# A two-layer hybrid trunk on one core: Toeplitz blocks written from their diagonal on, first GLU weights loaded early, S5 carries kept apart

## The chip, the cores and the metric

The program runs on one core of a Trainium2 chip. The metric is the device time of one execution in microseconds (us); lower is better. Three runs of the kernel before gave 1280.75, 1279.62 and 1279.68 us: median 1279.68 us.

The core has a matrix engine (PE, TensorE), a vector engine (DVE, VectorE), a scalar engine (ACT, ScalarE), a general engine (POOL, GpSimd) and SP (SyncE), which here only issues DMAs. ACT issues DMAs too, from the same instruction stream as its arithmetic. All DMAs share 16 DMA engines. The engines run their own instruction lists and wait for each other at semaphores.

## What is computed

x has 512 tokens of 1024 values. Layer 0 is an S5 mixer and a SwiGLU block, layer 1 a retention mixer and a SwiGLU block, with a norm before each. The change touches the S5 mixer alone:

```python
lam_bar = jnp.exp(lam * step)                      # 64 groups x 64 complex states
b_bar = ((lam_bar - 1.0) / lam)[..., None] * b
bu = jnp.einsum('blgn,gpn->blgp', uf, b_bar)       # uf: normed x, 64 groups of 16
_, states = lax.associative_scan(combine, (a, bu), axis=1)   # s[t] = lam_bar*s[t-1] + bu[t]
y = jnp.einsum('gnp,blgp->blgn', c, states).real + d * uf
y = jax.nn.gelu(y.reshape(bsz, seq, D_MODEL))
y = y * jax.nn.sigmoid(y @ glu_w + glu_b)
```

## The kernel before

**Tiling.** The 512 tokens are 64 chunks of 8 steps (`CH`, `STEPS`). The 64 groups sit as 32 pairs `j`, two groups to the 128 partitions. Within a chunk, the output is a product of the chunk's inputs `u` with a block Toeplitz matrix `toep`; what came before the chunk enters by the chunk's first state, `states`, times tables `r_tc`. So y = u x toep (`y_inputs`, L680) + states x tables (`y_states`, L660), both on PE, accumulated in one PSUM bank for each four pairs (k = 0 to 7).

**Toeplitz blocks.** PE makes the nonzero taps of four pairs at a time (`strips(k)`, L609 and L612). ACT copies them to `strip` in `w_raw` (`strip_out(k)`), behind seven steps of zeros that POOL wrote at the start (L1684). A row block r (16 partitions) of `toep` is the strip shifted by r steps. `toeplitz_half(queue, part, half)` (L427 to L436) waits until the two strips of a part are copied and issues eight DMAs, r = 0 to 7, each from 16 partitions to 16 partitions of SBUF with 4096 bytes a partition. SP does this for half 0, ACT for half 1, for four parts (0 to 3): 32 DMAs on each. `toep_loaded[part]` counts both halves.

**Scan.** DVE scans the 64 chunk states as 8 segments of 8 (L1368 to L1381; `seg_done` 1), carries the ends of the segments on (L1384 to L1400, 3 operations a segment; `seg_done` 2) and adds the carried ends to the seven inner states of each later segment, in four quarters of the pairs (L1403 to L1424, eight operations of 392 elements a quarter; `scan_done` 1 to 4). The powers for that come from POOL (`segment_powers`, `lift_ready`), between two of its seven table blocks (`tc_ready`).

**Order.** Each engine's list is written out by hand. ACT's list around the change: strips 0 and 1 out, DMAs of part 0, strips 2 and 3, eight copies to `xT`, DMAs of part 1, strips 4 and 5, DMAs of part 2, strip 6, the load of the Gelu table (L1007), strip 7, DMAs of part 3, then four Gelus (L1017), four `g_hi` copies, the first split of GLU weights `w_hi` (`split_weights(0, 0)`), and the second four of each. PE's list: y_inputs 0 to 3, y_states of quarter 0, y_inputs 4 and 5, y_states of quarter 1, transposes of y 0 to 3 (L672), y_inputs 6 and 7, y_states of quarters 2 and 3, transposes 4 to 7, and then the GLU products (L709 to L711), from which on PE goes through the rest of the network. The strips and the GLU weights share `w_raw`, so SP loads the first weights when all Toeplitz DMAs of a slot have landed. PSUM copies of the chunk states (`s5_input_out`) are written with the chunk as the innermost index, 256 bytes from element to element.

## Time and profile before

| what | us |
|---|---|
| median of three runs | 1279.68 |
| profiled execution | 1278.21 |
| its span on the core | 1276.4 |
| PE busy (matmul) | 1240.6 (97% of the span) |
| DVE busy | 671.7 (53%) |
| ACT busy | 462.0 (36%) |
| POOL busy | 64.8 (5%) |

The profiled execution is 1.8 us longer than its span: that lies before the first and after the last instruction. Busy time counts arithmetic only. A DMA that ACT or SP issues is not busy time, but the engine does nothing else while it issues; the timeline shows these under ACTq and SPq. "[1.46 <-DVE ...]" behind a row is the time that the engine stood idle before it and what ended that. The chain of waits follows the end of the program back from what released it to what released that; its rows are not a sum over an engine but one path in time. The granted clock is the share of full speed at which PE was let run: 1.00 is 2.4 GHz, 0.50 is 1.2 GHz.

### The profile page before, as it was taken

The numbers are of one execution on the slowest core, as the hardware profiler recorded it, in microseconds if no ns is written. First come the engines' busy times: TensorE is split into PE (matmuls) and PEld (weight loads), VectorE is DVE, ScalarE is ACT, GpSimd is POOL, SyncE is SP. The second block draws the span as 40 slices with busy tenths as digits, with TensorE's granted clock in tenths as the row PEclk, the third lists the DMA queues.
The fourth block names the chain that finished last, engine by engine and source line by source line (L and its number), as shares of the span: only waits on it lengthen the run. The fifth ranks groups of instructions, "written<-read, shape, count | busy, mean of one in ns | idle before, by whom it ended". The sixth has DMA issues, their size and how long they took to land.

```text
span 1276.4 us, 16013 instructions
## 1 busy us (share of the span) xinstructions
PE 1240.6 (97%) x6277; PEld 1034.5 (81%) x6277; DVE 671.7 (53%) x785; ACT 462.0 (36%) x486; POOL 64.8 (5%) x82
## 2 busy tenths in 40 slices
PE   3889999999999999999999999999999999999998
PEld 3778888888888888888888888888888888888886
DVE  8997754344444444646655465634454444444443
ACT  5635433333333333333333333422333333332232
POOL 6940000000000000000000000000000000000000
PEclk9999999999999999999999999999999999999999
DMA  5373333332312334323232133233232323323331
GB/s 115 100 144 123 99 99 99 99 99 90 105 58 90 105 90 138 107 66 107 66 99 83 57 107 96 69 96 93 74 119 80 102 94 99 99 68 90 93 110 66
DMA packets 141039, 121.03 MB, mean 95 GB/s; under 512 B 5720, under 2 KB 132880, under 8 KB 141008
## 3 DMA queue, kind: packets, MB, share of 16 engines
q1 hardware_dynamic: 138832, 116.40, 29.5%
q10 hardware_dynamic: 2176, 4.20, 1.7%
q8 instruction: 22, 0.36, 0.1%
q14 instruction: 9, 0.07, 0.0%
HBM read 114.29 MB, written 2.10 MB: 91 GB/s over the span
## 4 chain that ended last, share of the span: by engine, by line
PE 94%; ACTq 2%; ACT 2%; DMA 1%; DVE 1%; issue 0%; SPq 0%; DVEq 0%
PE bank L709 27%; PE bank L711 27%; PE bank L710 27%; PE bank L809 2%; PE bank L808 2%; PE bank L807 2%; ACTq L434 2%; DMA s<-in_x_dram 1%; PE bank L835 1%; PE bank L837 1%; PE bank L836 1%; PE bank L846 1%; PE bank L820 0%; PE bank L821 0%; ACT s_states L900 0%; PE bank L537 0%
## 5 line engine op out<-in xcount | busy, mean ns | idle before, releaser
L709 PE MATMUL bank<-u_hi,w_hi 128*128 128x512 f32 x960 | 374.9, 391 | 0.0
L711 PE MATMUL bank<-u_hi,w_lo 128*128 128x512 f32 x960 | 373.6, 389 | 0.0
L710 PE MATMUL bank<-u_lo,w_hi 128*128 128x512 f32 x960 | 373.5, 389 | 0.0
L1186 DVE TENSOR_TENSOR w_lo<-w_raw,w_hi 128x2048 fp32r<-128x2048 f32 x112 | 256.4, 2290 | 165.7 <-ACT w_hi L900 165.6
L900 ACT ACTIVATE w_hi<-w_raw 128x2048 fp32r<-128x2048 f32 x112 | 214.0, 1910 | 319.1 <-PE bank L711 314.0
L709 PEld LDWEIGHTS bank<-u_hi,w_hi 128*128 128x128 f32 x960 | 180.2, 188 | 37.8 <-issue 0.7
L710 PEld LDWEIGHTS bank<-u_lo,w_hi 128*128 128x128 f32 x960 | 180.2, 188 | 37.6 <-issue 0.5
L711 PEld LDWEIGHTS bank<-u_hi,w_lo 128*128 128x128 f32 x960 | 180.2, 188 | 37.5
L709 PE MATMUL bank<-h_hi,w_hi 128*128 128x512 f32 x352 | 136.9, 389 | 0.0
L710 PE MATMUL bank<-h_lo,w_hi 128*128 128x512 f32 x352 | 136.9, 389 | 0.0
L711 PE MATMUL bank<-h_hi,w_lo 128*128 128x512 f32 x352 | 136.9, 389 | 0.0
L1176 DVE TENSOR_TENSOR tmp<-bank,tmp 128x512 f32<-128x512 f32 (+3 forms) x60 | 38.0, 634 | 97.1 <-PE bank L711 94.3
L1092 ACT ACTIVATE tmp<-tmp 128x512 f32<-128x512 f32 x44 | 27.7, 632 | 138.9 <-DVE tmp L1525 138.0
L1525 DVE TENSOR_TENSOR tmp<-bank,tmp 128x512 f32<-128x512 f32 x44 | 30.0, 691 | 91.2 <-PE bank L711 90.7
L711 PEld LDWEIGHTS bank<-h_hi,w_lo 128*128 128x128 f32 x352 | 66.1, 188 | 13.8
L710 PEld LDWEIGHTS bank<-h_lo,w_hi 128*128 128x128 f32 x352 | 66.1, 188 | 13.7
L709 PEld LDWEIGHTS bank<-h_hi,w_hi 128*128 128x128 f32 x352 | 66.1, 188 | 13.7
L1451 DVE TENSOR_TENSOR xT<-bank,xT 128x512 f32 (+1 forms) x24 | 16.6, 692 | 92.5 <-PE bank L711 92.5
L1042 ACT ACTIVATE u_hi<-xT,vecs (+1 forms) x24 | 17.3, 721 | 124.4 <-DVE xT L1451 124.4
L709 PE MATMUL bank<-y_hi,w_hi 128*128 128x512 f32 x128 | 49.9, 390 | 0.0
L710 PE MATMUL bank<-y_lo,w_hi 128*128 128x512 f32 x128 | 49.8, 389 | 0.0
L711 PE MATMUL bank<-y_hi,w_lo 128*128 128x512 f32 x128 | 49.8, 389 | 0.0
(220 smaller groups left out, 1321.6 us busy)
## 6 DMA issues: line engine op xcount, KB each, us to landing
w_raw<-in_ret_w_qkvg_dram SPq DMA_DIRECT2D x24, 1024.0 KB, 4.9
w_raw<-in_ffn_w_gate_dram SPq DMA_DIRECT2D x22, 1024.0 KB, 5.2
w_raw<-in_ffn_w_up_dram SPq DMA_DIRECT2D x22, 1024.0 KB, 5.1
w_raw<-in_ffn_w_down_dram SPq DMA_DIRECT2D x32, 704.0 KB, 4.1
w_raw<-in_ret_w_o_dram SPq DMA_DIRECT2D x8, 1024.0 KB, 5.1
w_raw<-in_s_glu_w_dram SPq DMA_DIRECT2D x4, 1024.0 KB, 5.5
s<-in_x_dram ACTq DMA_DIRECT2D x8, 256.0 KB, 8.5
s_w<-in_x_dram SPq DMA_DIRECT2D x1, 2048.0 KB, 7.6
```

What stands on the lines that cost most here:

```text
L434: queue.dma_start(toep[N * r:N * r + N, half, part, :, :, :].rearrange("p t j n -> p (t j n)"), strip[row:row + N, part % 2, first:first + ...
L709: pe.matmul(o, w_hi[w][:, w_cols], hi, start=first, stop=False)
L710: pe.matmul(o, w_hi[w][:, w_cols], lo, start=False, stop=False)
L711: return pe.matmul(o, w_lo[w][:, w_cols], hi, start=False, stop=end)
L807: pe.matmul(o, a_hi, w_hi[s][:, cols], start=(kk == 0), stop=False)
L808: pe.matmul(o, a_hi, w_lo[s][:, cols], start=False, stop=False)
L809: mm = pe.matmul(o, a_lo, w_hi[s][:, cols], start=False, stop=(kk == KT - 1))
L900: return act.activation(o, i, ACT.Copy, scale=scale)
L1092: act.activation(sig[:, m, :], sig[:, m, :], ACT.Silu).then_inc(gate_ready, 1)
L1176: return dve.tensor_tensor(o, a, b, ALU.mult)
L1186: dve.tensor_tensor(w_lo[s][:, :], w_raw[:, s, :], w_hi[s][:, :].bitcast(F32), ALU.subtract).then_inc(w_lo_ready[s], 1)
L1525: dve.tensor_tensor(sig[:, m, :], bank[m][:, :], rs, ALU.mult).then_inc(bank_free[m], 1)
```

## The change

It has these parts.

1. `toeplitz_half` sends the strip from the diagonal on: row block r takes 8 - r steps, 4096 - 512 r bytes a partition. What lies before the diagonal is zeroed by seven DMAs of SP from a row of zeros that POOL writes (`zeros`, in slot 0 of `w_raw`), before the token load. The strips now all lie in slot 1.
2. Slot 0 of `w_raw` is free once the zeros have landed, so SP loads the first GLU weights there right behind the token load. ACT's first split moves up to between the table load and strip 7.
3. DVE keeps the carried segment ends in a tile of its own, `carries`. ACT copies the first of them (`carry0_ready`; DVE waits for it before the lift) and copies the other six back into `states` (`ends_ready`; PE waits for it before `y_states`).
4. The lift of a quarter is one product of 392 elements, one of 784 and two additions of 784. POOL makes its two tables (`lift_pair`), two more operations of 224 elements in `segment_powers`.
5. PE: y_inputs 4 ahead of y_states of quarter 0; y_inputs 6 and 7 ahead of transposes 0 to 3. DVE's making of `step64` moves ahead of the scan. `s5_input_out` writes four pairs side by side, 16 bytes at a stretch.

ACT's list from behind the DMAs of part 2 to the first Gelu, before (`s_1` is `toep`, `s_3` holds `carries`, the 32x8x64 copies are `strip_out`):

```order
L900 ACTIVATE w_raw<-bank 32x8x64 [waits bank_full4]
L1007 ACT_TABLE_LOAD
L1007 ACTIVATE small<-eps 128x1
L900 ACTIVATE w_raw<-bank 32x8x64 [waits bank_full5]
L434 DMA s_1<-w_raw 16x1024 [waits bank_free5,bank_free4]
L434 DMA s_1<-w_raw 16x1024 x7
L1017 ACTIVATE y_chunk<-bank 128x4x8x16 [waits bank_full6]
```

The same place now, up to the second of the eight DMAs of part 3:

```order
L920 ACTIVATE s_3<-s_states 128x4x16 [waits seg_done]
L920 ACTIVATE w_raw<-bank 32x8x64 [waits bank_full4]
L1028 ACT_TABLE_LOAD
L1028 ACTIVATE small<-eps 128x1
L920 ACTIVATE w_hi<-w_raw 128x2048 [waits w_loaded0]
L920 ACTIVATE s_states<-s_3 128x6x32 [waits seg_done]
L920 ACTIVATE s_states<-s_3 128x6x32
L920 ACTIVATE w_raw<-bank 32x8x64 [waits bank_full5]
L444 DMA s_1<-w_raw 16x1024 [waits bank_free5,bank_free4]
L444 DMA s_1<-w_raw 16x896
```

Four instructions came in ahead of the DMAs of part 3: the copy of the first carry, the split of the weights, and the two copies of the carried ends.

PE's list from y_states of quarter 1 to y_inputs 6, before (L672 transposes a finished y, L680 is `y_inputs`, L660 `y_states`):

```order
L660 MATMUL bank<-s_tc,s_states 64x128 [waits scan_done]
L660 MATMUL bank<-s_tc,s_states 64x128 x31
L672 MATMUL bank<-ident,y_chunk 128x128 [waits bank_free6,bank_free7]
L672 MATMUL bank<-ident,y_chunk 128x128 x3
L672 MATMUL bank<-ident,y_chunk 128x128 [waits bank_free7]
L672 MATMUL bank<-ident,y_chunk 128x128 x3
L672 MATMUL bank<-ident,y_chunk 128x128 [waits bank_free2,bank_free3]
L672 MATMUL bank<-ident,y_chunk 128x128 x3
L672 MATMUL bank<-ident,y_chunk 128x128 [waits bank_free3]
L672 MATMUL bank<-ident,y_chunk 128x128 x3
L680 MATMUL bank<-s_1,s_u 64x128 [waits bank_free4,toep_loaded3]
L680 MATMUL bank<-s_1,s_u 64x128 x7
```

And now, from y_inputs 4 on (L699 is `y_inputs`, L679 `y_states`, L691 the transposes):

```order
L699 MATMUL bank<-s_1,s_u 64x128 [waits toep_loaded2,seg_done]
L699 MATMUL bank<-s_1,s_u 64x128 x7
L679 MATMUL bank<-s_tc,s_states 64x128 [waits scan_done,ends_ready]
L679 MATMUL bank<-s_tc,s_states 64x128 x31
L699 MATMUL bank<-s_1,s_u 64x128 x8
L679 MATMUL bank<-s_tc,s_states 64x128 [waits scan_done,ends_ready]
L679 MATMUL bank<-s_tc,s_states 64x128 x31
L699 MATMUL bank<-s_1,s_u 64x128 [waits bank_free4,toep_loaded3]
L699 MATMUL bank<-s_1,s_u 64x128 x7
L699 MATMUL bank<-s_1,s_u 64x128 [waits bank_free5]
L699 MATMUL bank<-s_1,s_u 64x128 x7
L691 MATMUL bank<-ident,y_chunk 128x128 [waits bank_free6,bank_free7]
```

The wait for part 3 of the Toeplitz blocks now stands ahead of the transposes 0 to 3 as well.

The diff (the new semaphores, the waits of PE for `ends_ready` and `toep_zeroed`, and the renamed views of `step64` and `carry_tmp` are left out):

```diff
-        strip = w_raw[0:4 * N, :, 0:(2 * STEPS - 1) * PART * N].rearrange("p s (t j n) -> p s t j n", t=2 * STEPS - 1, j=PART)
-        scan_tmp = r_3[:, 4096:8192]
+        strip = w_raw[0:4 * N, 1, :].rearrange("p (s t j n) -> p s t j n", s=2, t=STEPS, j=PART)
+        zeros = w_raw[0:N, 0, 0:(STEPS - 1) * PART * N]
+        lift_pair = powers[:, :, :, :].rearrange("p r t j -> p (r t j)")[:, 0:2 * (SEG - 1) * J] \
+            .rearrange("p (i r j) -> p i r j", i=SEG - 1, r=2)
+        carries = r_3[:, 4096:4544].rearrange("p (q s r j) -> p q s r j", q=4, s=SEG - 1, r=2)
+        carry_diff = r_3[:, 4544:4768].rearrange("p (q s j) -> p q s j", q=4, s=SEG - 1)
+        lifted_diff = r_3[:, 4768:5160].rearrange("p (s i j) -> p s i j", s=SEG - 1, i=SEG - 1)
+        lifted = r_3[:, 5160:5944].rearrange("p (s i r j) -> p s i r j", s=SEG - 1, i=SEG - 1, r=2)
+        seg = states[:, 1:CH + 1, :, :].rearrange("p (s i) r j -> p s i r j", s=SEG)
+        seg_ends = seg[:, :, SEG - 1, :, :].rearrange("p s r (q j) -> p s q r j", q=4)
 
...
                 queue.wait_ge(bank_free[b], fill + 1)
             row = 2 * N * (part // 2) + N * half
             for r in range(STEPS):
-                first = STEPS - 1 - r
-                queue.dma_start(toep[N * r:N * r + N, half, part, :, :, :].rearrange("p t j n -> p (t j n)"),
-                                strip[row:row + N, part % 2, first:first + STEPS, :, :].rearrange("p t j n -> p (t j n)")
+                queue.dma_start(toep[N * r:N * r + N, half, part, r:, :, :].rearrange("p t j n -> p (t j n)"),
+                                strip[row:row + N, part % 2, 0:STEPS - r, :, :].rearrange("p t j n -> p (t j n)")
                                 ).then_inc(toep_loaded[part], 16)
 
         @block.sync
                 n = vec.shape[0] // P
                 sp.dma_start(vec_rows[col:col + n, :], vec.rearrange("(k p) -> k p", p=P)).then_inc(vecs_loaded, 16)
 
+            sp.wait_ge(zeros_set, 1)
+            b, fill = S5_AT[("u", 7)]
+            sp.wait_ge(bank_full[b], fill + 1)
+            for r in range(1, STEPS):
+                cols = r * PART * N
+                sp.dma_start(toep[N * r:N * r + N, :, :, 0:r, :, :].rearrange("p h q t j n -> p (h q) (t j n)"),
+                             repeated(zeros[:, 0:cols], 1, 2 * NPART)).then_inc(toep_zeroed, 16)
+
             b, fill = S5_AT[("tb", 4 * NTAB - 1)]
             sp.wait_ge(bank_full[b], fill + 1)
             sp.dma_start(x_tok, x[0].rearrange("(t p) d -> p t d", p=P)).then_inc(x_loaded, 16)
 
-            sp.wait_ge(pads_zeroed, 1)
+            sp.wait_ge(toep_zeroed, 16 * (STEPS - 1))
+            load_unit(0, 0, glu_v[:, :, 0:256], KT, 256)
             for part in range(NPART):
                 toeplitz_half(sp, part, 0)
-            for s in range(2):
-                for part in (s, 2 + s):
-                    sp.wait_ge(toep_loaded[part], 16 * 2 * STEPS)
-                load_unit(s, 0, glu_v[:, :, 256 * s:256 * s + 256], KT, 256)
+            for part in range(NPART):
+                sp.wait_ge(toep_loaded[part], 16 * 2 * STEPS)
+            load_unit(1, 0, glu_v[:, :, 256:512], KT, 256)
             for s in range(2):
                 load_unit(s, 1, glu_v[:, :, 512 + 256 * s:768 + 256 * s], KT, 256)
 
...
             pe.wait_ge(seg_done, 2)
-            y_states(0, 0)
             pe.wait_ge(toep_loaded[2], 16 * 2 * STEPS)
             y_inputs(4)
+            y_states(0, 0)
             y_inputs(5)
             y_states(1, 1)
-            for k in range(4):
-                y_transposed(k)
             pe.wait_ge(toep_loaded[3], 16 * 2 * STEPS)
             y_inputs(6)
             y_inputs(7)
+            for k in range(4):
+                y_transposed(k)
             y_states(2, 4)
             y_states(3, 5)
             for k in range(4, 8):
...
             def s5_input_out(k):
                 ps, free = s5_full("b", k)
-                copy(states[:, 1:CH + 1, :, JB * SLOT[k]:JB * SLOT[k] + JB].rearrange("p c r j -> p j r c"),
-                     ps[:, :].rearrange("p (j r c) -> p j r c", j=JB, r=2)).then_inc(free, 1)
+                copy(states[:, 1:CH + 1, :, JB * SLOT[k]:JB * SLOT[k] + JB],
+                     ps[:, :].rearrange("p (j r c) -> p c r j", j=JB, r=2)).then_inc(free, 1)
...
-            act.wait_ge(pads_zeroed, 1)
             toeplitz_half(act, 0, 1)
             strip_out(2)
             strip_out(3)
...
             strip_out(4)
             strip_out(5)
             toeplitz_half(act, 2, 1)
+            act.wait_ge(seg_done, 1)
+            copy(carries[:, :, 0], seg_ends[:, 0]).then_inc(carry0_ready, 1)
             strip_out(6)
             act.activation(small[:, 25:26], eps[:, :], ACT.Gelu_apprx_tanh)
+            split_weights(0, 0)
+            act.wait_ge(seg_done, 2)
+            for ri in range(2):
+                copy(seg[:, 1:SEG - 1, SEG - 1, ri, :].rearrange("p s (q j) -> p s q j", q=4),
+                     carries[:, :, 1:SEG - 1, ri, :].rearrange("p q s j -> p s q j")).then_inc(ends_ready, 1)
             strip_out(7)
             toeplitz_half(act, 3, 1)
 
...
 
-            dve.wait_ge(lift_ready, 1)
+            dve.wait_ge(lift_ready, 2)
             rotation(step8, seg_powers[:, :, 0, :])
+            last_lift = seg_powers[:, :, SEG - 1, :].rearrange("p r (q j) -> p r q j", q=4)
+            step(dve.tensor_copy(step64[:, 0], repeated(last_lift[:, 0], 2, 2)))
+            step(dve.tensor_copy(step64[:, 1, :, 0], last_lift[:, 1]))
+            step(dve.tensor_scalar(step64[:, 1, :, 1], last_lift[:, 1], -1.0, None, ALU.mult))
+            settle()
 
             dve.wait_ge(state0_ready, 1)
...
             last.then_inc(seg_done, 1)
             dve.wait_ge(seg_done, 1)
 
-            rotation(step64, seg_powers[:, :, SEG - 1, :])
-            w = step64[:, :, :, :].rearrange("p a r j -> p a (r j)")
             for n in range(1, SEG - 1):
-                old = seg[:, n - 1, SEG - 1, :, :].rearrange("p r j -> p (r j)")
-                now = seg[:, n, SEG - 1, :, :]
-                step(mul(carry_tmp, repeated(old, 1, 2), w))
-                settle()
-                flat = now.rearrange("p r j -> p (r j)")
-                step(dve.tensor_tensor(flat, flat, carry_tmp[:, 0, :], ALU.add))
-                settle()
-                last = dve.tensor_tensor(now, now, carry_tmp[:, 1, :].rearrange("p (r j) -> p r j", r=2)[:, ::-1, :],
-                                         ALU.add)
+                if n == 1:
+                    for a in range(2):
+                        step(mul(carry_tmp[:, a], seg_ends[:, 0], step64[:, a]))
+                else:
+                    step(mul(carry_tmp, repeated(carries[:, :, n - 1], 1, 2), step64))
+                settle()
+                step(dve.tensor_tensor(carries[:, :, n], seg_ends[:, n], carry_tmp[:, 0], ALU.add))
+                settle()
+                last = dve.tensor_tensor(carries[:, :, n], carries[:, :, n], carry_tmp[:, 1][:, :, ::-1, :], ALU.add)
                 if n < SEG - 2:
                     step(last)
                     settle()
             last.then_inc(seg_done, 1)
             dve.wait_ge(seg_done, 2)
+            dve.wait_ge(carry0_ready, 1)
+            step(dve.tensor_tensor(carry_diff, carries[:, :, :, 0, :], carries[:, :, :, 1, :], ALU.subtract))
+            settle()
 
             JH, M = J // 4, SEG - 1
             for part in range(4):
                 js = slice(JH * part, JH * part + JH)
-                t = [[scan_tmp[:, (2 * ri + i) * M * M * JH:(2 * ri + i + 1) * M * M * JH].rearrange(
-                    "p (s i j) -> p s i j", s=M, i=M) for i in range(2)] for ri in range(2)]
-                carry = [repeated(seg[:, 0:M, SEG - 1, ri, js], 2, M) for ri in range(2)]
-                lift = [repeated(seg_powers[:, i, 0:M, js], 1, M) for i in range(2)]
-                for i in range(2):
-                    for ri in range(2):
-                        step(mul(t[ri][i], carry[ri ^ i], lift[i]))
-                settle()
-                for ri in range(2):
-                    into = seg[:, 1:SEG, 0:M, ri, js]
-                    step(dve.tensor_tensor(into, into, t[ri][0], ALU.add))
-                settle()
-                for ri in range(2):
-                    into = seg[:, 1:SEG, 0:M, ri, js]
-                    last = dve.tensor_tensor(into, into, t[ri][1], ALU.add if ri else ALU.subtract)
-                    if not ri:
-                        step(last)
-                settle()
-                last.then_inc(scan_done, 1)
+                step(mul(lifted_diff, repeated(carry_diff[:, part], 2, M), repeated(seg_powers[:, 1, 0:M, js], 1, M)))
+                step(mul(lifted, repeated(carries[:, part], 2, M), repeated(lift_pair[:, :, :, js], 1, M)))
+                settle()
+                into = seg[:, 1:SEG, 0:M, :, js]
+                step(dve.tensor_tensor(into, into, repeated(lifted_diff, 3, 2), ALU.add))
+                settle()
+                dve.tensor_tensor(into, into, lifted, ALU.add).then_inc(scan_done, 1)
                 dve.wait_ge(scan_done, part + 1)
 
             def y_low(k):
...
-                last.then_inc(lift_ready, 1)
-                pool.wait_ge(lift_ready, 1)
+                step(last)
+                settle()
+                pool.wait_ge(tb_ready, 1)
+                lift = [seg_powers[:, i, 0:SEG - 1, :] for i in range(2)]
+                pool.tensor_tensor(lift_pair[:, :, 0, :], lift[0], lift[1], ALU.subtract).then_inc(lift_ready, 1)
+                pool.tensor_tensor(lift_pair[:, :, 1, :], lift[0], lift[1], ALU.add).then_inc(lift_ready, 1)
+                pool.wait_ge(lift_ready, 2)
 
             for n, k in enumerate(POOL_BLOCKS):
                 if n == 1:
```

## Rows read from the trace of the kernel before

**Rows 1.** Busy time by stretch: start:end us, length, busy us, granted clock, DMA

```profile
80.50:101.60 21.10, 17.15 (x367) 15.57 (x366) 19.63 (x35) 11.79 (x20) 0.00 (x0) 1.00 0.73 168
101.60:1276.40 1174.80, 1168.45 (x5241) 969.65 (x5239) 580.85 (x608) 404.20 (x383) 0.00 (x0) 1.00 0.29 93
...
59.70:62.80 3.10, 0.02 (x1) 0.00 (x0) 2.98 (x4) 0.69 (x2) 3.02 (x3) 1.00 0.99 169
...
64.60:68.00 3.40, 3.40 (x18) 2.75 (x16) 3.26 (x5) 2.19 (x4) 3.32 (x4) 0.50 0.62 101
```

**Rows 2.** Chain of waits, 74 to 103 us: start, length, engine and line

```profile
81.17 1.28 ACT L1007
...
89.50 1.59 ACT y_chunk L1017 x3
...
91.13 1.97 PE bank L672 x16
93.11 1.97 PE bank L680 x32
95.08 4.14 PE bank L660 x123
...
101.86 0.23 PE bank L709
```

**Rows 3.** ACT's timeline, 50 to 97 us: start, length, what, idle before

```profile
52.18 1.99 ACT L900 ACTIVATE s_states<-bank 128x512 f32<-128x512 f32 x2 [0.80 <-PE bank L551]
55.33 0.59 ACT L900 ACTIVATE w_raw<-bank 32x512 f32<-32x512 f32 x1 [1.16 <-PE bank L612]
56.02 6.05 ACTq L434 DMA_DIRECT2D s<-w_raw  x8
...
69.02 5.00 ACTq L434 DMA_DIRECT2D s<-w_raw  x8
...
75.21 5.30 ACTq L434 DMA_DIRECT2D s<-w_raw  x8
...
83.35 6.10 ACTq L434 DMA_DIRECT2D s<-w_raw  x8
...
95.58 1.93 ACT L900 ACTIVATE w_hi<-w_raw 128x2048 fp32r<-128x2048 f32 x1 [1.70 <-DMA w_raw<-in_s_glu_w_dram]
```

**Rows 4.** SP's timeline, 0.5 to 16 us: DMA issues of other sizes

```profile
1.65 0.43 SPq L452 DMA_DIRECT2D s<-in_s_log_step_dram  x1
...
13.13 0.42 SPq L467 DMA_DIRECT2D s_d_diag<-in_s_d_dram  x1
...
15.33 0.32 SPq L472 DMA_DIRECT2D s<-in_ret_gn_w_dram  x1
```

**Rows 5.** Issue to landing of the L434 DMAs, 69.0 to 74.2 us

```profile
DMA to landing us min/median/max: 2.2/2.4/2.9
```

**Rows 6.** The same, 83.3 to 90 us

```profile
DMA to landing us min/median/max: 2.5/3.5/4.3
```

**Rows 7.** DMA issues, page part 6: x count, KB, us to landing

```profile
s_w<-in_x_dram SPq DMA_DIRECT2D x1, 2048.0 KB, 7.6
```

**Rows 8.** POOL's timeline, 25 to 80 us

```profile
25.88 0.73 POOL L1728 TENSOR_TENSOR s_c_powers<-s_c_powers,xT 128x256 f32<-128x256 f32 x1
...
77.17 1.27 POOL L1782 TENSOR_TENSOR s_tc<-s_pool_tmp,s_seg_tmp 128x512 f32<-128x512 f32 x1
```

**Rows 9.** PE's timeline, 79 to 84 us

```profile
79.28 1.93 PE L609 MATMUL bank<-s_tc,s_fb 128*32 128x128 f32 x16
...
83.03 1.20 PE L660 MATMUL bank<-s_tc,s_states 64*64 64x128 f32 x32 [1.46 <-DVE s_states L1419]
```

**Rows 10.** DVE's timeline, 45 to 83 us

```profile
54.30 1.23 DVE L1176 TENSOR_TENSOR bank<-s_states,bank 128x1024 f32<-128x1024 f32 x1 [1.78 <-ACT s_states L900]
...
74.28 0.22 DVE L1394 TENSOR_TENSOR s_states<-s_states,bank 128x64 f32<-128x64 f32 x1
...
78.73 2.00 DVE L1176 TENSOR_TENSOR s<-s_states,s_seg_powers 128x392 f32<-128x392 f32 x4
80.76 1.04 DVE L1415 TENSOR_TENSOR s_states<-s_states,s 128x392 f32<-128x392 f32 x2
81.84 1.04 DVE L1419 TENSOR_TENSOR s_states<-s_states,s 128x392 f32<-128x392 f32 x2
```

19 lines of the change are left out of this document (10 added, 9 removed).

## The prediction

> **What bounds the kernel.** I first read busy time by stretch. From 101.6 us to the end PE is busy 1168.45 of 1174.80 us, and none of the changed code runs there [rows 1]. So the change is worth what it moves the first GLU product, at 101.86 us on the chain [rows 2]. Then I read the chain of waits backwards from there: before that product stand PE's transposes, y_states, y_inputs 6 and 7 and transposes 0 to 3, in one piece from 91.13 us on, and before those ACT's first Gelu at 89.50 [rows 2]. That Gelu waits for nobody. ACT comes to it from its eight DMA issues of part 3, 83.35 to 89.45. Its timeline shows such bursts one after the other from 56.02 on: 6.05, 5.00, 5.30 and 6.10 us, with copies of 0.59 us between them [rows 3]. So ACT's instruction list, and in it 22.45 us of DMA issue, sets the time. DVE's scan is second: its first quarter released PE at 83.03, after 1.46 us of idle time [rows 9].
>
> **The bursts.** The change keeps 32 issues on ACT but sends 4096 - 512 r bytes a partition, 2304 on average. The question is whether an issue gets cheaper with its bytes. Burst 1 (of 0 to 3) ran alone, and there an issue takes 5.00 / 8 = 0.625 us with its gap of 0.03. Of issues from HBM with 16 partitions, one of 2048 bytes a partition took 0.42 us and one of 512 bytes 0.32 [rows 4]. Against that, the 64 single words of log_step cost 0.43 [rows 4], so bytes can't be all of it. The bounds are 0.35 an issue with its gap (every issue like the 512-byte one) and 0.625 (nothing falls). I take a straight line from 0.32 at 512 bytes to 0.60 at 4096: 0.46 at 2304 bytes, 0.49 with the gap, 3.9 us a burst, since the three rows of 16 partitions lie near one line. The other three bursts ran beside SP's and took 1.05, 0.30 and 1.10 us more than 5.00 [rows 3]. With fewer bytes under way I keep half: 0.5, 0.15 and 0.55. New bursts: 4.4, 3.9, 4.1, 4.5 us, 16.9 in place of 22.45.
>
> The Trainium skill ("DMA: Bandwidth & Descriptors", Rules for kernel authors) says that under 64 KB a transfer pays mostly overhead. These carried 64 KB and now carry less, so by it the bursts hardly shorten; the result is rival 1 below. The trace bears it out in part: a lone DMA took 2.4 us to land at the median whatever its 0.6 us of issue [rows 5].
>
> **ACT's list, step by step.** I count the time of each step on the old clock.
> - The chunk-state copies, two in 1.99 us, write one word every 256 bytes; ordinary ones of 512 columns take 0.59 [rows 3]. Now they write 16 bytes at a stretch: between 0.59 and 1.0 each. I take 0.6. The last two wait for PE in part, so strip 1 comes out 0.2 earlier: burst 0 from 55.8 to 60.2.
> - Strips 2 and 3 are made by PE in about 2.2 us each (1.93 plus the diagonal) [rows 9] and now wait for POOL. POOL's two added operations have 224 columns; one of 256 took 0.73 [rows 8], so 1.4 us for both, and every later table block is 1.4 late. Strip 3 is out at about 61.3. The eight xT copies took 6.2 us to burst 1 before; burst 1 runs from 67.5 to 71.4.
> - Strip 5 is out at 72.4, burst 2 ends at 76.5. The copy of the first carry (64 columns) is 0.25: 76.8. Strip 6: 77.4. Table load and the small Gelu behind it, 1.5 (1.28 of it in [rows 2]): 78.9. The moved split of 1.93 [rows 3]: 80.9. Two copies of 192 columns, 0.33 each: 81.6.
> - Strip 7 is now POOL's: its last table ended at 78.44 [rows 8], now 79.85; PE needs 2.2, ACT copies at 82.1 to 82.7. Burst 3: 82.7 to 87.2 (before: 89.45).
>
> **What replaces the wait for Gelu.** PE now needs part 3 landed before y_inputs 6, and the transposes stand behind it. The last issue starts at 86.7. Landing took 3.5 us at the median of the last burst, beside SP [rows 6], and 2.4 alone [rows 5]; with the bytes down I take 2.4: 89.1. From there PE has the same pieces as from 91.13 to 101.86 [rows 2], only in another order: 10.7 us. First product at 99.8 to 99.9, 1.9 to 2.0 us earlier.
>
> **What must not be late.** DVE: `step64` moves into the 1.78 us in which DVE waited for the states [rows 10], which hides its 0.5. The chain of carries (0.22 for an addition of 64 columns [rows 10]) ends near 77.9, after carry 0 (76.8), so no new wait. A quarter took 4.25 us (82.99 - 78.73: four products in 2.00, four additions in 2.08 and the gaps) [rows 10]. 392 columns are 0.5 and 784 about 0.95, so 0.5 + 3 x 0.97 and gaps is 3.5: quarters end at 81.8, 85.3, 88.8, 92.3 (before the last at 95.7). y_states of quarter 0 waits for strip 7 and y_inputs 4 on PE, until 83. The last quarter is wanted at about 93, so DVE is off the path, by under 1 us. SP: seven zero DMAs carry 1.8 MB, 28 times a strip block; at 0.6 us for each block they last from about 34 to 51, ahead of the token load. The token load (7.6 us to landing [rows 7]) starts at 50.4 behind their tail and now has 1 MB of weights behind it. It is wanted at 61.3 and I expect it near 60. If it slips, each us goes on the path. The moved split costs 1.93 here and frees as much at 95.58, where ACT was waiting [rows 3], so it pays nothing back.
>
> **Sum.** Bursts -5.5, copies of states -0.2, added on ACT +2.8 (0.25 + 1.93 + 0.65), waits for POOL and PE that replace part of the gain +0.7, landing and the new order +0.3: -1.9 us. The profiled execution goes from 1278.21 to 1276.3; on the median of 1279.68 that is 1277.8. The bound of what I can tell from no change is 0.2%, 2.6 us: this forecast lies within it.
>
> **Rivals.**
> 1. An issue costs the same whatever its bytes, and the meetings with SP stay. For it: all the log_step words at 0.43, like much larger ones. Then burst 2 ends at 80.3, and carry 0 at 80.55 holds DVE back by 2.6 us, which then ends at 95. Strip 7 is out at 85.9, burst 3 ends at 91.9, landing is 93.7, the product 104.5: +2.6 us, 1282.3. This is the side of slower, and it decides from 0.6 us an issue on: four instructions of 2.8 us stand in a list that has no slack. It has an addition. PE would then stand idle about 3 us before y_inputs 6. After 3.10 us with 0.02 busy (59.7 to 62.8) PE's granted clock was 0.50, that is 1.2 GHz, from 64.6 to 68.0 [rows 1]; 3.4 us at half clock is up to 1.7 us of work: 1284.0 at most. Shorter idle times, 1.46 us at 83.03 [rows 9], were followed by a granted clock of 1.00 [rows 1].
> 2. An issue costs the same alone, but SP and ACT no longer get in each other's way: bursts of 5.0. That is 2.45 us less than rival 1: +0.2 us, 1279.9.
> 3. More than I took: issues near 0.35, bursts of 2.8 to 3. Strip 7 still waits for POOL until 82.1, so only burst 3 gains beyond the forecast, 1.5 us, and then DVE's last quarter at 92.3 holds PE: about -3 us, 1276.7.
> 4. The change doesn't bring early weights: the token load and the zeros hold SP until past 62. Each us late adds one; and PE had waited 3.1 us there before [rows 1], so up to about 1 us of slip is covered. It would lift the forecast to about 1279.5.
>
> **Chances and range.** Forecast 0.42, rival 1 0.26, rival 2 0.14, rival 3 0.13, rival 4 0.05. Inside the forecast the time is 1276.5 to 1279, by the half of the meetings that I kept and by landing. Faster by over 0.2% (below 1277.1): all of rival 3 and two fifths of the forecast, 0.30. Slower by over 0.2% (above 1282.2): some four fifths of rival 1, 0.21. The rest, 0.49, is no change that could be told. Range 1275.6 to 1283.0: it leaves out the worst of rival 1 with the lower clock, and a gain above rival 3.
>
> **What would show it.** The row of L444 on ACTq: bursts near 4 us and single issues that fall from r = 0 to r = 7 (forecast), flat at 0.6 (rivals 1 and 2). DVE's idle time before the 224-column subtraction: none, or 2.6 us by `carry0_ready` (rival 1). PE's wait before y_inputs 6 should be named `toep_loaded`'s DMA, and be under 2 us. Quarters of 3.5 us on DVE: if the four-index additions run slower than 0.97 for 784 columns, by a third, the last quarter ends at 95 and DVE is the bound after all. The GLU part from the first product to the end should take what it took, 1276.4 - 101.9 = 1174.5 us; if it doesn't, my premise that all lies before it is wrong.

## The result, and the profile after

| | median us | lowest to highest | runs |
|---|---|---|---|
| before | 1279.65 | 1277.23 to 1283.04 | 20 |
| after | 1282.61 | 1278.97 to 1285.54 | 20 |

The ratio is 1.0019, with a 95% interval of 1.0012 to 1.0025: slower by 1.5 to 3.2 us (the medians differ by 2.96), which is measured, though the ratio lies just within the 0.2% that the prediction called no change. The forecast was 1277.8. Rival 1 of the prediction had 1282.3.

The two profiled executions differ by more than the medians do. That of after took 1284.40 us, 1.8 above its median, that of before [rows 1] 1278.21, 1.4 below. So of the 6.2 us between the two traces some 3.2 are spread, and a difference of one or two us between two traces proves nothing here.

Busy time by stretch in the trace after (start:end, length, busy us of PE, PEld, DVE, ACT and POOL, granted clock, DMA share, GB/s):

```profile
96.20:99.70 3.50, 3.50 (x33) 3.33 (x34) 0.88 (x1) 0.00 (x0) 0.00 (x0) 0.54 0.68 218
107.85:1282.60 1174.75, 1168.38 (x5241) 969.91 (x5239) 580.74 (x608) 404.22 (x383) 0.00 (x0) 1.00 0.29 92
```

From the first GLU product to the end it took 1174.75 us, as before [rows 1]. The same stretch had 1174.7 to 1174.9 in the traces of the experiments. So that premise held, and all that follows happens before 108 us.

The chain of waits after (start, length, engine and line; L444 is the DMA issue of the strips, L699 `y_inputs`, L691 the transposes, L679 `y_states`):

```profile
70.84 0.46 ACTq L444
...
71.33 0.61 ACTq L444
...
75.18 0.61 ACTq L444
...
82.31 0.26 ACT s L920
...
82.59 0.59 ACT w_raw L920
...
83.20 1.28 ACT L1028
...
84.70 1.80 ACT w_hi L920
86.50 0.51 ACT s_states L920 x2
...
87.03 0.60 ACT w_raw L920
...
93.28 2.88 DMA s<-w_raw
...
96.20 3.50 PE bank L699 x32
99.71 1.90 PE bank L691 x16
101.60 3.85 PE bank L679 x125
```

The issues from 70.84 to 75.18 are burst 1, r = 0 to 7: 0.61 us at 3584 bytes a partition and 0.61 at 512. Against [rows 2], the four added instructions of ACT now stand on the chain, then part 3's landing, and then PE works off `y_inputs` 6 and 7 at about half its clock (0.54), in 3.50 us for 1.97 [rows 2].

ACT's timeline after, against [rows 3]:

```profile
54.18 0.60 ACT L920 ACTIVATE s_states<-bank 128x512 f32<-128x512 f32 x1 [0.34 <-PE bank L569]
56.40 0.59 ACT L920 ACTIVATE w_raw<-bank 32x512 f32<-32x512 f32 x1 [1.62 <-PE bank L630]
57.07 6.83 ACTq L444 DMA_DIRECT2D s<-w_raw  x8
...
70.79 5.00 ACTq L444 DMA_DIRECT2D s<-w_raw  x8
...
77.00 5.27 ACTq L444 DMA_DIRECT2D s<-w_raw  x8
...
87.70 6.38 ACTq L444 DMA_DIRECT2D s<-w_raw  x8
```

Bursts of 6.83, 5.00, 5.27 and 6.38 us are 23.5 in all: 22.45 before, 16.9 predicted. The whole list lies late: strip 1 comes out at 56.40 (before at 55.33), burst 3 starts at 87.70 (before at 83.35, predicted 82.7). PE and DVE wait for it. Their rows after, DVE's first:

```profile
82.67 0.39 DVE L1429 TENSOR_TENSOR s<-s 128x224 f32<-128x224 f32 x1 [3.74 <-ACT s L920]
```

```profile
50.17 0.57 PE L569 MATMUL bank<-s_u,s 128*64 128x64 f32 x12 [1.01 <-issue]
...
87.05 2.12 PE L679 MATMUL bank<-s_tc,s_states 64*64 64x128 f32 x64 [2.07 <-ACT s_states L920]
...
96.20 3.50 PE L699 MATMUL bank<-s,s_u 128*64 128x128 f32 x32 [3.87 <-DMA s<-w_raw]
```

DVE stood 3.74 us for the first carry, PE 2.07 us for the copied ends and 3.87 us for the landing of part 3. The stand of 1.01 us at 50.17 has no releaser; it is taken up below.

### The profile page after: what moved, and what is told of

Its sections match the earlier page's. It is cut to its first block, busy times and chain, and to the rows that moved or that the text cites. A ratio compares the mean times of both kernels' runs of the same rounds, so it can differ in the third digit from the quotient of the medians.

```text
span 1282.6 us, 16013 instructions
## 1 busy us (share of the span) xinstructions
PE 1241.9 (97%) x6277; PEld 1036.1 (81%) x6277; DVE 668.9 (52%) x771; ACT 459.9 (36%) x489; POOL 65.3 (5%) x83
## 4 chain that ended last, share of the span: by engine, by line
PE 94%; ACTq 2%; DMA 1%; ACT 1%; DVE 1%; issue 0%; SPq 0%; DVEq 0%
PE bank L729 27%; PE bank L731 27%; PE bank L730 27%; PE bank L827 2%; PE bank L828 2%; PE bank L829 2%; ACTq L444 2%; DMA s<-in_x_dram 1%; PE bank L856 1%; PE bank L857 1%; PE bank L855 1%; PE bank L866 1%; PE bank L569 0%; PE bank L555 0%; PE bank L840 0%; PE bank L841 0%
## 5 line engine op out<-in xcount | busy, mean ns | idle before, releaser
L829 PE MATMUL bank<-w_hi,u_lo 128*128 128x512 f32 x128 | 49.8, 389 | 0.0
L827 PE MATMUL bank<-w_hi,u_hi 128*128 128x512 f32 x128 | 49.8, 389 | 0.0
```

The source lines that it names most:

```text
L827: pe.matmul(o, a_hi, w_hi[s][:, cols], start=(kk == 0), stop=False)
L829: mm = pe.matmul(o, a_lo, w_hi[s][:, cols], start=False, stop=(kk == KT - 1))
```

## The experiments

Each kernel ran 10 to 12 times (run 7 seven times, run 8 four), beside the kernel before on the same chip (its medians there were 1279.91 to 1280.09 us). A ratio's interval is some 0.1% to either side, 1.2 us. So a single step under 1.5 us isn't told apart, and each such step is given below with that reserve. Between two kernels whose times both spread over 5 us or more, as those near the change do, even 2 us can be chance. "The lift alone" is the kernel of the sixth run, from which many others start.

**Parts taken back from the changed kernel.** Run 1 puts ACT's weight split back behind the copies of `g_hi`.

```
-            split_weights(0, 0)          # behind the small Gelu
+            split_weights(0, 0)          # behind the four y_high(k)
```

> The changed kernel, with ACT's first split of GLU weights (1.89 us in its trace) back behind the four g_hi copies; the rest as changed. Theory A (ACT's instruction list sets the time, and an issue costs about 0.61 us whatever its bytes): the fourth burst of Toeplitz issues starts 1.8 to 1.9 us earlier after the copy of strip 1 than in the changed kernel, and the first GLU product follows; if PE's idle time before y_inputs 6 falls from 3.9 us to about 2 its granted clock may also stay at 1.00, worth up to 1.5 more. About 1280.7 us, 1279.2 at best. Theory B (the zero DMAs and the early weights slow the Toeplitz DMAs, and that is the loss): first burst still 6.8 us, time as the changed kernel, 1282.6.

1282.18 us, ratio 1.0019 [1.0008, 1.0029]. Nothing to be told from the 1282.61 of the change: taking back the split alone doesn't bring the loss back. Its 12 times spread over 6.6 us, so a share of up to about 2 us isn't excluded.

Run 2 is the kernel before with the zero DMAs and the short rows alone.

> The kernel before, with one part of the change alone: seven zero DMAs ahead of the token load, and Toeplitz transfers of 4096 - 512 r bytes a partition. No early weights, ACT's and PE's lists as before. Theory A: each issue stays at 0.61 us on ACT and 0.59 on SP, four bursts of 5.0 to 6.5 us, time as the kernel before within 0.5 us (1279.65). Theory B: the first burst is over 6.5 us and the time 1 us or more above it. My recorded forecast (issues get cheaper with their bytes) would give bursts near 4 us and 2 us less than before.

1280.1 us, 1.0003 [0.9995, 1.0012]: the part from which 5.5 us were to come brought none. What of that is the short rows and what the zero DMAs, this run doesn't tell; run 13 does.

Run 3 is run 1 with DVE making the copies of the first carry and of the ends, so that nothing is added to ACT ahead of burst 3.

```
-            copy(carries[:, :, 0], seg_ends[:, 0]).then_inc(carry0_ready, 1)     # ACT
...
+            step(dve.tensor_copy(carries[:, :, 0], seg_ends[:, 0]))
...
```

> The changed kernel, with nothing added to ACT ahead of the last burst: the split is back behind the g_hi copies, and DVE itself copies the first carry and the six carried ends (three operations, about 0.9 us). Theory A: ACT's list between the copy of strip 1 and the first Gelu is that of the kernel before, so the last burst ends as far behind that copy as there (33.5 us or so), DVE's four quarters end 2 us earlier than before and nothing is gained by it, since ACT is the path; y_inputs 6 waits for its landing: 1279.9 us, between before and 0.5 above. Theory B: 1 us or more above before. A theory C (the order on PE costs: the transposes 0 to 3 now wait for the landing of part 3) would leave it 1 to 2 us above before as well, with PE idle before y_inputs 6.

1281.68 us, 1.0014 [1.0005, 1.0023]: 0.9 less than the change, which can't be told from nothing. With the rest of the change in place, taking away all of ACT's additions still leaves it slower than before.

Run 4 is the changed kernel with TensorE's transposes 0 to 3 ahead of `y_inputs` 6 again.

> The changed kernel, with PE's transposes 0 to 3 ahead of y_inputs 6 and 7 again, as in the kernel before. Theory A: the last burst ends as in the changed kernel, the transposes (2.0 us) run while part 3 lands, so that y_inputs 6 starts at the landing and the first GLU product comes 1.5 to 2 us earlier; with less idle time PE's clock may stay up, 1.5 more: 1280.7, or 1279.3. Theory that the new order on PE is harmless since the chain has the same pieces either way: no change, 1282.6.

1282.36 us, 1.0021 [1.0011, 1.003]. No difference. In its trace PE waits for another thing instead, the Gelu, which stands behind burst 3 (ending at 93.07):

```profile
94.75 1.97 PE L691 MATMUL bank<-ident,y_chunk 128*128 128x128 f32 x16 [1.44 <-ACT y_chunk L1043]
96.64 1.97 PE L699 MATMUL bank<-s,s_u 128*64 128x128 f32 x32
```

**The lift by itself.** Run 5 is run 3 with late first weights and the transposes 0 to 3 ahead of `y_inputs` 6 again.

> The kernel of e3_copies_on_dve, with the first GLU weights loaded behind the Toeplitz DMAs as in the kernel before, and PE's transposes 0 to 3 ahead of y_inputs 6 again. What is left of the change is the zero DMAs, the diagonal transfers, the lift, the carries and the chunk-state copies. Theory B1 (the early weights' 1 MB, under way with part 0, lengthen the first burst): first burst back to about 6.0 us and time 1280.0. Theory B2 (the zero DMAs do it by holding the token load up to 61 us): first burst stays at 6.5, time about 1281. Theory C (PE's order) also gives 1280.0; the first burst tells B1 and C apart.

1281.66 us, 1.0014 [1.0005, 1.0023]. It tells little: with all strips in slot 1 the weights wait for all four parts here, and in its trace their landing came onto the path.

Run 6 has of the change only the lift, its tables and carries, `step64` moved and the state copies in stretches of 16 bytes. Transfers and weights are those of before, PE's transposes 0 to 3 stand ahead of `y_inputs` 6 as before, and DVE makes the copies. One thing of PE's new order stays in it, and in all runs that start from it: `y_inputs` 4 ahead of `y_states` of quarter 0. So its gain can't be given to the lift alone.

> The kernel before, with the DVE and POOL side of the change alone: carries apart with DVE making its own copies, the three-product lift, step64 ahead of the scan, the chunk-state copies of 16 bytes a stretch, POOL's two table operations. Toeplitz transfers of 4096 bytes with the zeros in the strip, late weights, PE's order as before. Theory A (ACT's list is the path): bursts as before, DVE's four quarters take 14.0 us and not 17.0 and end 2 us earlier, which nobody uses but y_states of quarter 0; 1279.5, within 0.5 of before. If DVE were on the path after all, it would be 2 us faster.

1277.93 us, 0.9984 [0.9975, 0.9993]: faster than both kernels. Its chain:

```profile
78.58 1.24 POOL s_tc L1793
79.83 0.04 issue
79.87 1.93 PE bank L618 x16
81.81 0.36 PE bank L621 x8
...
82.19 0.60 ACT w_raw L910
```

POOL's last table releases strip 7, as the prediction had it, at 79.83 (79.85 predicted).

**What an issue's price hangs on.** Runs 7 and 8 join parts 0 and 1 in DMAs of 128 KB, eight instead of sixteen on each queue, with ACT's eight behind the `xT` copies; in run 8 SP issues ACT's share as well.

```
+            for r in range(STEPS):
...
+                queue.dma_start(toep[N * r:N * r + N, half, 0:2, :, :, :].rearrange("p q t j n -> p q (t j n)"),
+                                strip[row:row + N, 0:2, first:first + STEPS, :, :].rearrange("p q t j n -> p q (t j n)")
...
```

> The kernel of e6_lift_alone, with fewer issues and the same bytes: parts 0 and 1 lie side by side in toep and in the strips, so one DMA carries both (16 partitions, two stretches of 4096 bytes, 128 KB). ACT and SP issue 24 each in place of 32; ACT's burst for parts 0 and 1 stands behind the xT copies. PE's strips 6 are ahead of y_inputs 0. Theory A (what costs is the number of issues): the first burst of ACT is gone, PE's wait for bank 6 (3.1 us) falls under 1, ACT's last burst starts at about 81.7 and not 83.4, held by POOL's last table and PE's strips 7; the first GLU product 1.5 to 2 us earlier: 1278.0. If an issue is paid by bytes after all, the double DMAs take 1.2 us each and the time is that of before.

> The kernel of e7_pair_one_burst, with SP issuing both halves of parts 0 and 1 (16 DMAs), so that ACT issues 16 in all and not 24. Theory A: 5 us less on ACT; ACT then comes to strip 7 before PE has made it, and POOL's last table (about 79.8), PE's strips 7 and the copy become the bound: last burst from about 82, so the same time as e7_pair_one_burst, 1278.0, at best 0.5 less. If ACT's list were still the path there it would be 3 us less.

1283.66 us, 1.0031 [1.0019, 1.0043], and 1293.43 us, 1.0107 [1.0092, 1.0123]: both slower. In run 7 ACT's eight took 10.12 us, what two lone bursts of 5.00 take. SP's issues on the chain of run 8:

```profile
68.82 1.25 SPq L455
...
71.39 1.25 SPq L455
...
72.68 1.19 SPq L455
...
73.92 1.96 SPq L455
```

A DMA of 128 KB from 16 partitions took 1.19 to 1.27 us to issue behind others of its kind, twice the 0.61 of one of 64 KB: 105 GB/s. (The 1.96 us stood beside a burst of ACT.) The first three of run 8 took 0.74, 0.62 and 0.59 us, so 128 KB alone are no dearer to issue; the price rises once others are under way. A joined DMA also has twice as many stretches, but that isn't it: the seven zero DMAs of run 9 below have 128 stretches each, and SP issued those of 64 to 256 KB in 0.60 to 0.74 us and those of 320, 384 and 448 KB behind them in 1.75, 2.52 and 3.17. So 64 KB lie about where two prices meet, a floor of 0.61 us below and the pace of the data above. Neither fewer bytes nor fewer DMAs helped there. The Trainium skill ("SBUF — State Buffer", Door 1: The DMA port swizzle) says that DMA bandwidth depends on how many of the 16 SBUF ports the partitions reach; by its formula 16 partitions reach 4, a quarter of its 436 GB/s, an estimate of 109. The 105 here agrees.

**The zero DMAs and the two copies.** Run 9 adds the seven zero DMAs to the lift alone; full rows go over them later.

> The kernel of e6_lift_alone (the fastest so far, 1277.9), with the seven zero DMAs of the change added and nothing else: the Toeplitz transfers are still 4096 bytes and write over them. Theory B (the zero DMAs are what the change costs): they keep the DMA engines full from 34 to 54 us; PE stands about 1 us near 48 us with no engine to wait for (as in the traces of the changed kernel and of e5_late_weights), and the token load lands 3 us later, beside the first burst, which gets longer. 2 to 3 us more: 1280 to 1281. Theory A (ACT's list alone): no effect, 1277.9.

1281.9 us, 1.0014 [1.0005, 1.0023]: 4.0 more than the 1277.93 without. In its trace the token load too is late, landing 13.1 us after its issue (run 6: 8.7), and PE waits for it:

```profile
65.12 5.18 PE L657 MATMUL bank<-ident,s_w 128*128 128x128 f32 x24 [4.16 <-DMA s_w<-in_x_dram]
```

Run 10 is the changed kernel without them (the area before the diagonals isn't written: that part of the computation is left out).

> The changed kernel without the seven zero DMAs: what lies before the diagonals of toep is left as it was, so that part of the computation is left out. Theory B: no stand of PE near 48 us, the token load lands by 58 to 60, first burst nearer 6; 2 to 3 us less than the changed kernel: 1280. Theory A (the four instructions added to ACT's list cost it all): as the changed kernel, 1282.6.

1282.1 us, 1.0015 [1.0006, 1.0024]: only 0.5 less than the change. The two runs don't fit a plain sum.

Run 11 is the kernel before with the state copies alone, run 12 the lift alone with ACT making the copies.

```
-                copy(states[:, 1:CH + 1, :, JB * SLOT[k]:JB * SLOT[k] + JB].rearrange("p c r j -> p j r c"),
-                     ps[:, :].rearrange("p (j r c) -> p j r c", j=JB, r=2)).then_inc(free, 1)
+                copy(states[:, 1:CH + 1, :, JB * SLOT[k]:JB * SLOT[k] + JB],
+                     ps[:, :].rearrange("p (j r c) -> p c r j", j=JB, r=2)).then_inc(free, 1)
```

> The kernel before, with one edit: ACT's eight copies of chunk states write four pairs side by side (0.60 us a copy and not 1.0). My prediction gave it 0.2 us. If it is the main gain in e6_lift_alone (whose first strips came out 0.9 us earlier), it is about 1 us: 1279.0, with strip 0 out at about 45.5 us and not 46.3. If the gain there came from the lift and the carries, this run is at 1279.9.

> The kernel of e6_lift_alone, with ACT copying the carried ends as the changed kernel has it (first carry behind the second-part burst, the other six behind the Gelu table; DVE waits for the first). Theory A: 0.85 us more in ACT's list, of which the 0.74 us that ACT waits for strip 7 there hides most, but y_states of quarter 0 and the last quarter come later: DVE starts its lift about 80.0 and not 79.9. So 1278.0 to 1278.8. If the wait of DVE for ACT is what costs in the changed kernel, it is 1 us or more over e6_lift_alone.

1278.9 us, 0.9991 [0.9982, 1.0], and 1279.51 us, 1.0001 [0.9991, 1.0012]. So ACT's copies cost 1.6 us against run 6, at the edge of what is told apart. In run 11 the state copies fall from 1.0 to 0.60 us each. ACT's rows in run 11:

```profile
51.04 0.60 ACT L900 ACTIVATE s_states<-bank 128x512 f32<-128x512 f32 x1 [0.80 <-PE bank L551]
51.98 0.60 ACT L900 ACTIVATE s_states<-bank 128x512 f32<-128x512 f32 x1 [0.34 <-PE bank L551]
54.19 0.59 ACT L900 ACTIVATE w_raw<-bank 32x512 f32<-32x512 f32 x1 [1.62 <-PE bank L612]
```

Strip 1 comes out at 54.19 for 55.33 [rows 3], 1.1 us earlier and not 0.2, since the pairs of such copies ahead of it got shorter too (strip 0 comes out at 45.53 for 46.34).

**Settling what was open.** Run 13 is the lift alone with short rows and no zeros (that area isn't written).

> The kernel of the run with the lift alone (1277.9 us), with one edit: the 64 transfers carry only what lies from the diagonal on (512 to 4096 bytes a partition instead of 4096); no zero DMAs are added, so the area before the diagonals keeps what was there: that part of the computation is left out. Theory A (an issue has a price of about 0.6 us whatever its bytes): the lone second burst stays at 5.00 us, every burst within 0.2 us of 5.0 where it stands alone, and the time stays at 1277.9 within 1 us. Theory B (my prediction's: 0.49 us by bytes, so 1.1 us a burst): the second burst 3.9 us, the whole 2 to 4 us faster, near 1275. Theory C (the shorter rows themselves cost time, through the landing or the GLU weights that collide with them): slower than 1279.

1278.6 us, 0.9995 [0.9986, 1.0004]. ACT's bursts:

```profile
68.07 5.00 ACTq L442 DMA_DIRECT2D s<-w_raw  x8
74.27 5.28 ACTq L442 DMA_DIRECT2D s<-w_raw  x8
82.85 6.43 ACTq L442 DMA_DIRECT2D s<-w_raw  x8
```

With 56% of the bytes they are those of the full rows, to 0.01 us (in run 6: 5.00, 5.28 and 6.43); the first one, beside the token load, took 6.62 for 6.44. With all else fixed, the smaller size is worth nothing.

Run 14 is run 3 without the zeros (area not written), so the change without all that was added to ACT and to the DMA queues.

> The changed kernel with three parts taken back: ScalarE's weight split stands behind the copies of g_hi again, VectorE makes the copies of the carried ends, and the zero DMAs are gone (the area before the diagonals keeps what was there: that part of the computation is left out). What is left of the change: short rows, lift, early first weights, the new order on TensorE. If the parts add (zero DMAs +4.0 as in the run that added them to the lift alone, from 1281.7 with them), 1277.7 us. If the zero DMAs only cost what taking them from the changed kernel gave (0.5), 1281.2. If the early weights or the new order of TensorE cost something by themselves, it lies in between: 1279 to 1280.5.

1279.97 us, 0.9996 [0.9987, 1.0005]. With ACT's additions gone the zeros do show, by 1.7 us (1281.68 in run 3). In run 10 they hardly did (0.5), and why isn't shown: in its trace burst 3 starts 29.3 us behind strip 1 for 31.3 in the changed kernel's, but then lasts 8.02 us for 6.38. The zeros and ACT's additions taken away together, from the change to run 14, are worth 2.6 us, which is clear of the spread; either one alone, 0.5 and 0.9, is not.

Run 15 moves the making of `lift_pair` from POOL to DVE and makes DVE's copies as `tensor_tensor` max of a thing with itself.

> The kernel with the lift alone (1277.9 us), where GpSimd's last table (end 79.8) releases the last strip, and where VectorE's three copies took 1.12 and 2.19 us beside GpSimd. Edits: VectorE makes the two products' table lift_pair (GpSimd 1.4 us less), and makes its copies as tensor_tensor max of a thing with itself. Theory A (GpSimd's last table sets the last burst, copies are slow by their form): copies 0.22 and 0.7 us, last table 1.4 us earlier, burst 3 starts at 81.4 instead of 82.86, time 1276.5. Theory B (the copies are slow by their data or their place): copies stay near 1.1 and 2.2, VectorE's last quarter ends later than TensorE needs it, time 1278. Theory C: the earlier last burst only meets SyncE's transfers and lasts longer, as the bursts of 5.8 to 8.0 us did: no change, 1277.9.

1279.84 us, 0.9996 [0.9987, 1.0005]: 1.9 slower than the lift alone. POOL was done 1.4 us earlier, yet its trace has burst 3 at 83.38 instead of 82.86: ACT's list, behind xT copies that waited for a PE at half clock, now released it. The copies did get shorter. Run 6's, then run 15's:

```profile
71.62 1.12 DVE L1398 COPY s<-s_states 128x64 f32<-128x64 f32 x1
...
77.75 2.19 DVE L1415 COPY s_states<-s 128x192 f32<-128x192 f32 x2
```

```profile
72.39 0.28 DVE L1398 TENSOR_TENSOR s<-s_states 128x64 f32<-128x64 f32 x1
...
77.69 1.25 DVE L1416 TENSOR_TENSOR s_states<-s 128x192 f32<-128x192 f32 x2
```

A copy of 64 columns took four times as long as the same work as a two-input operation, both beside a busy POOL. The Trainium skill ("SBUF — State Buffer", Who interferes with whom) says that a copy in a two-port mode and a GpSimd instruction block each other, the later one until the earlier has ended. The trace agrees as far as it goes: run 6's first copy ended at 72.74, POOL's operation beside it at 72.69. The page says that two inputs from SBUF contend with GpSimd's reads as well, and of that these rows show less. Which mode the copies were in no run shows.

Run 16 is run 9 with the zeros by block column.

```
-            for r in range(1, STEPS):
...
-                sp.dma_start(toep[N * r:N * r + N, :, :, 0:r, :, :].rearrange("p h q t j n -> p (h q) (t j n)"),
...
+            for t in range(STEPS - 1):
+                sp.dma_start(toep[N * (t + 1):, :, :, t, :, :].rearrange("p h q j n -> p (h q) (j n)"),
...
```

> The run that added the seven zero DMAs to the lift alone (1281.9 us, +4.0 over 1277.9), with the same bytes (1.8 MB) written by block column over 112 to 16 partitions at a time instead of by block row into 16 partitions each. Theory A (the zeros cost by lying in 16 partitions for 20 us, under TensorE's instruction fetch, the token load and ScalarE's first burst): each of the large ones lands in some 3 to 5 us, all by about 42 us, the distance from strip 0 to strip 1 falls from 9.9 back to 8.65 us, the token load takes 7.6 us, time 1278 to 1279. Theory B (any 1.8 MB there cost it, or the wait of the transfers on them): as before, 1281 to 1282.

1277.86 us, 0.9987 [0.9978, 0.9996]: all of the 4.0 us are regained, with the same bytes. Stretches of run 9, then of run 16:

```profile
32.00:44.00 12.00, 10.88 (x185) 9.94 (x184) 10.53 (x10) 11.19 (x22) 11.54 (x15) 1.00 0.63 76
44.00:54.00 10.00, 8.56 (x167) 7.63 (x167) 9.37 (x18) 5.79 (x11) 9.37 (x18) 1.00 0.96 110
```

```profile
32.00:44.00 12.00, 10.89 (x185) 9.76 (x184) 11.30 (x10) 11.30 (x24) 11.57 (x14) 1.00 0.75 154
44.00:54.00 10.00, 9.70 (x183) 8.77 (x182) 9.60 (x19) 5.56 (x10) 9.37 (x18) 1.00 0.29 103
```

By rows of 16 partitions the DMA engines are 0.96 busy from 44 to 54 us and move only 110 GB/s; PE does 1.1 us less work there. By columns they move 154 GB/s ahead of 44 and are mostly free behind (0.29). The time from issue to landing, run 9 and run 16:

```profile
DMA to landing us min/median/max: 2.4/6.5/12.8
```

```profile
DMA to landing us min/median/max: 4.6/5.5/6.6
```

Run 17 is the changed kernel with that one edit, run 18 is run 14 with PE's old order (area not written).

> The changed kernel with one edit: its seven zero DMAs write the same bytes by block column over 112 to 16 partitions, which took the 4.0 us away where they had been added to the lift alone (1277.9). Theory A (the parts add): 4 us less than the changed kernel's 1282.6, so 1278.6. Theory B (the zeros lie partly beside ScalarE's added copies and split, which hold the last burst in any case, as when the zeros were left out of the changed kernel and 1282.1 came out): 1281 to 1282. Either way strip 1 follows strip 0 by 8.65 us instead of 9.9.

> The run without zero DMAs and without ScalarE's added work (1280.0 us) with TensorE's old order (transposes 0 to 3 ahead of y_inputs 6); the area before the diagonals keeps what was there: that part of the computation is left out. Against the run with short rows alone (1278.6) only the early first weights and the strips' place are left. Theory A (the new order costs: TensorE stands before y_inputs 6 with nothing to do): 1278.6. Theory B (the early weights cost, by lying under the first burst): 1280.0. Theory C (neither; the 1.4 us are the spread of two medians): between, within 0.7 of 1279.3.

1281.83 us, 1.0012 [1.0003, 1.0021], and 1277.87 us, 0.9984 [0.9975, 0.9993]. So the edit doesn't repair the change, as run 10 had it already. And PE's new order costs 2.1 us in the medians where ACT isn't late: run 14 with it 1279.97, run 18 without it 1277.87. The early weights, with the strips all in slot 1, cost nothing to be told (run 13: 1278.6). PE in run 14, then in run 18:

```profile
91.69 1.97 PE L691 MATMUL bank<-s,s_u 128*64 128x128 f32 x32 [2.56 <-DMA s<-w_raw]
93.58 1.97 PE L683 MATMUL bank<-ident,y_chunk 128*128 128x128 f32 x16
```

```profile
91.04 3.17 PE L683 MATMUL bank<-ident,y_chunk 128*128 128x128 f32 x16 [1.91 <-ACT y_chunk L1027]
94.15 2.38 PE L691 MATMUL bank<-s,s_u 128*64 128x128 f32 x32
```

In the old order the transposes stand in the time in which part 3 is landing. At full clock that is worth less than the medians say: from the end of ACT's last burst to the first GLU product it takes 11.8 us in the old order (runs 5, 12 and 13) and 11.4, 12.5 and 13.1 in the new (runs 1, 3 and 14), as the landing goes, so at most 1.3 more. Run 18's profiled execution took 1279.38 us, 1.5 above its median, and had a granted clock of 0.50 from 91.6 to 95.0 us; run 14's took 1278.36, 1.6 below its median, and had 1.00 there. So these two traces don't show the difference of the medians. Whether a low clock made the rest in run 14's other executions isn't shown: the mean clock of a whole execution was 0.998 in its four fastest and 0.996 to 0.998 in the other seven, but 0.997 in the five fastest of run 18.

## Why the prediction was wrong

Medians, from the kernel before to the changed one, each line with one part more:

| kernel | us | step |
|---|---|---|
| before | 1279.9 | |
| state copies (run 11) | 1278.9 | -1.0 |
| + lift, DVE's copies, `y_inputs` 4 first (run 6) | 1277.9 | -1.0 |
| + short rows (run 13) | 1278.6 | +0.7 |
| + early weights, strips in slot 1 (run 18) | 1277.9 | -0.7 |
| + `y_inputs` 6 and 7 ahead of the transposes (run 14) | 1280.0 | +2.1 |
| + zero DMAs (run 3) | 1281.7 | +1.7 |
| + copies on ACT (run 1) | 1282.2 | +0.5 |
| + the split moved up (after) | 1282.6 | +0.4 |

The steps depend on their order. The -2.0 down to the lift and the +3.8 from run 18 to run 3 are beyond their uncertainty, steps under 1.5 us are not. None of the steps is the gain of 5.5 us that the forecast rested on.

- **The step that failed: the bursts, that is, the cost of an issue.** The prediction drew a line from 0.32 us at 512 bytes to 0.60 at 4096, from loads out of HBM, and got 16.9 us of issue. It measured 23.5, and 0.61 for each lone issue from 8 to 64 KB. The log_step row [rows 4], which it named as the evidence against itself, was the better guide. So was the rule of the Trainium skill that it quoted ("DMA: Bandwidth & Descriptors", Rules for kernel authors); this trace agrees, with 0.61 us at 8 KB. With that step's 5.5 us gone, its own sum gives 1283.3 on the medians, and rival 1, which also reworked the waits, 1282.3. That this lies 0.3 from the measured time is partly luck: rival 1 put the zero DMAs at nothing and PE's order at next to nothing, and its +2.6 us come from ACT's additions, of which taking them away (run 3) gave back 0.9.
- **Meetings with SP.** Half of them was to go with the bytes. Run 13 against run 6: nothing went.
- **The zero DMAs, put at nothing.** They cost 1.7 to 4.0 us where ACT isn't late. The prediction looked only at SP's queue and the token load. It missed that transfers into 16 partitions fill the DMA engines (a share of 0.84 to 0.98 from 36 to 54 us in the trace after). In all six traces with the lift and the zeros by rows PE stood for 0.9 to 1.3 us, up to 48.5 to 50.4 us, with no releaser named, and strip 1 came 9.8 to 10.2 us behind strip 0. In those with the zeros by columns or without zeros PE had no such stand, and strip 1 came 8.65 us behind, 8.99 with the old state copies. That the stand is PE's instructions coming late over the same queues was not tested.
- **Landing and order, +0.3.** Costed by the pieces of work, which came out right. But the time in which part 3 lands has nothing to cover it in the new order. Runs 14 and 18 put 2.1 us on it, of which traces at full clock show at most 1.3. In the changed kernel (run 4) it costs nothing to be told; there the old order waits for Gelu.
- **State copies, -0.2: too small.** -1.0 in the medians (run 11), within the uncertainty, and strip 1 1.1 us earlier in its trace.
- **Added on ACT, +2.8: the size was right** (0.26 + 1.80 + 0.51 on the chain, 2.6). In the medians it is only 0.9, within the uncertainty; where the rest of it went isn't shown.
- **Right:** quarters of 3.5 us on DVE; POOL's two operations 1.4 us late and strip 7 behind them (run 6: 79.83); DVE's wait for carry 0, given as 2.6 in rival 1, measured 3.74; PE's idle time ahead of `y_inputs` 6, given as 3, measured 3.87, and behind it a granted clock of 0.54 for 3.5 us, that is, 1.2 GHz for most of it. PE's work in it took 1.5 us longer than in [rows 2], of the 1.7 allowed. The length of a wait alone doesn't tell whether the clock falls: behind waits of 3.83 and 4.09 us (runs 17 and 10) it was low too, but behind 3.30 (run 5) it was 1.00 and behind 1.91 (run 18) 0.50.

Which part of the spread, 6.6 us in the changed kernel, comes from low clocks and which from the meetings with SP (ACT's last burst took 5.8 to 8.0 us in the traces) stays open, and so does how the zeros and ACT's additions share the 2.6 us that they cost together.

The version to keep is run 6, the lift alone: 2.0 us less than before, 4.7 less than the change. Run 16 ties with it, and its zeros do nothing there.

## What to carry to other kernels

Before counting on smaller DMAs, find in the same trace two of the same kind (same route, same partitions) with different bytes; if only others are there, take the flat price as the forecast and the gain as the rival. Shape a fill or a broadcast over many partitions: the same 1.8 MB cost 4 us by rows of 16 partitions and nothing by columns. Where an engine must wait for a landing, leave it the work that needs nothing from it, and count as the price of a bare wait also a clock that may be low behind it.

## What the runs showed of the hardware

- DMAs between 16 partitions of SBUF: 0.61 us an issue on ACT and 0.59 on SP from 8 to 64 KB; at 128 KB 0.59 to 0.74 us for the first three and 1.19 to 1.27 behind them: a floor, and a pace of 105 GB/s.
- The same bytes to 112 down to 16 partitions: landed within 6.6 us each, where rows of 16 partitions took up to 12.8.
- DVE's copies of 64 and 192 columns, beside a busy POOL, 1.12 and 1.10 us; as operations with two inputs, 0.28 and 0.63.
- ACT's copies from PSUM with stretches of 4 bytes 1.0 us, with 16 bytes 0.60, for the same 512 columns.
